# Norm of x at the head of an encoder block: transposing it by products with a scaled diagonal, squares on two engines, a TensorE run on zeros

## The chip, the core and the metric

The kernel runs on one core of one Trainium2 chip. The metric is the device time of one execution in microseconds. A core has five engines with instruction streams of their own: PE (TensorE, matmuls; its weight loads are shown as PEld), DVE (VectorE), ACT (ScalarE), POOL (GpSimd) and SP (SyncE, which here only issues DMAs). They meet in semaphores. SBUF is the on-chip memory of 128 partitions, PSUM (the tensor `ps`, 8 banks of 512 columns) takes what PE writes.

## What is computed

One encoder block for 256 tokens of width 2048, with 16 meta tokens put in front (272 rows, `L`): a norm, one wide projection, a state-space mixer and an attention mixer, their merge, and a feed-forward part that gathers rows of two tables for each token. What matters here is its first step:

```python
def rms_norm(x, g):
    xf = x.astype(jnp.float32)
    y = xf * lax.rsqrt(jnp.mean(xf * xf, axis=-1, keepdims=True) + NORM_EPS)
    return (y * g.astype(jnp.float32)).astype(x.dtype)

    hs = jnp.concatenate([meta, x], axis=1)
    h = rms_norm(hs, norm_mix[l])
    z = h @ w_in[l]
```

## The kernel before

**Layout.** x lies with tokens on the partitions: `xn` holds two halves of 128 tokens (t = 0, 1) with 2048 columns each, and the meta tokens are 16 rows of `xs`. The projection needs h turned round, with the model width on the partitions: 16 blocks `k` of 128 columns, each [128, 272]. It is needed in two parts, `hH` (rounded to what the fast matmul mode takes) and `hL` (the rest), so that three fast matmuls do the work of an exact one; weights are split in the same way into `high_slot(n)` and `low_ring`.

**The roots.** ACT squares the meta rows, the first half and the second half of x, each 2048 wide, and adds up in the same instruction (lines 480 to 487). DVE's `factors` makes the mean, ACT the root, DVE's `rstd` the reciprocal with one step of refinement: once for the meta rows and the first half together, once for the second half. DVE multiplies each half with its factor into `xs` (lines 880, 882), ACT the meta rows (line 491).

**The turn.** PE turns `xs` block by block: a transposition of the 16 meta rows (line 1321) and one for each half (line 1323), with `ident`, the identity of 128 x 128, into bank k % 4 of `ps`. ACT copies the bank to `hH` with the norm's weights (line 496), DVE makes `hL` of the bank and `hH` (line 887). A bank comes free when DVE is through with it.

**The first weights.** SP loads meta, the two halves of x, all parameters `prm` (128 x 1240, `ident` in their midst), and then weight tiles of 1 MB into a ring of four. ACT's `high(n)` (line 474) copies a ring slot rounded, DVE's `low(n)` (line 792) makes the rest; for tile 0 POOL does (line 401, `s_first`). ACT runs `high(0)` ahead of the turn and `high(1)` behind it. Then POOL makes two copies of h for later (lines 406, 407). PE's `split_product` (lines 1308 to 1310) takes 48 matmuls of 272 columns for a tile of 16 blocks and adds one to `s_wdone`, which SP's further loads and ACT's further `high` wait for.

**The order** is the order of the code on each engine; there is no scheduler. Programs of the engines wait for semaphore counts, written `wait_ge`. `step` on DVE makes an instruction wait for the one before.

Of the kernel before, what the change touches and what calls it, by code (L numbers as in the profile page):

```python
# [38 lines left out]
RING = 4  # L39
NEG = -3.0e38  # L40
# [25 lines left out]
def build(nc, W, keys, par, bw, cw, meta, x, gffn, gfin, u_tab, v_tab, out):  # L66
    top = ExitStack()
    with top:
        def sem(name):
            return top.enter_context(nc.semaphore(name))  # L70
# [24 lines left out]
        st = sbt(top, "st", [P, 16])  # L95
        halfpi = sbt(top, "halfpi", [P, 1])
# [66 lines left out]
        xs = gates[:, 0:3 * D].rearrange("p (t d) -> p t d", t=3)  # L163
        squares = [a[:, :, :].rearrange("p k t -> p (k t)") for a in (ybT, yT)]
# [65 lines left out]
        s_par = sem("s_par")  # L230
# [8 lines left out]
        s_sq, s_ms, s_sqr, s_xs = sem("s_sq"), sem("s_ms"), sem("s_sqr"), sem("s_xs")  # L239
        s_meta, s_xsm, s_gv = sem("s_meta"), sem("s_xsm"), sem("s_gv")  # L240
# [104 lines left out]
        def _(sp):  # L345
# [8 lines left out]
            sp.dma_start(xs[0:META, TT, :], meta).then_inc(s_x[TT], 16)  # L354
            for t in range(TT):
                sp.dma_start(xn[:, t, :], x[t * P:(t + 1) * P, :]).then_inc(s_x[t], 16)
            sp.dma_start(prm[:, :], par).then_inc(s_par, 16)
# [39 lines left out]
        def _(pool):  # L397
            pool.sem_inc(s_msum, 2)

            pool.wait_ge(s_high, 1)  # L400
            pool.tensor_tensor(low_ring[:, 0, :], ring[:, 0, :], high_slot(0), ALU.subtract).then_inc(s_first, 1)

            pool.wait_ge(s_hL, 4 + KT)
            pool.wait_ge(s_xs, TT)
            pool.wait_ge(s_sq, 3)
# [52 lines left out]
        def _(act):  # L458
            act.sem_inc(s_hT, 4)
# [20 lines left out]
            nc.scalar.activation(squares[0][0:META, :], xs[0:META, TT, :], ACT.Square, accum_out=st[0:META, 1:2]).then_inc(s_sq, 1)  # L480
            act.wait_ge(s_x[0], 16)
# [283 lines left out]
        def _(dve):  # L765
# [8 lines left out]
            dve.sem_inc(s_hL, 4)  # L774
# [9 lines left out]

            step(nc.vector.memset(halfpi[:, :], HALF_PI))
            step(nc.vector.memset(magic[:, :], MAGIC))
            nc.vector.memset(st[:, :], 1.0).then_inc(s_ms, 1)

            def low(n, i=0):

                dve.wait_ge(s_high, nth_high(n) + 1 + RING * i)
# [3 lines left out]
            def discretise():  # L795

                dve.wait_ge(s_par, 16)
# [62 lines left out]
            def rstd(dst, ss, v, root):  # L860
# [4 lines left out]
                step(nc.vector.tensor_scalar(ss, ss, -0.5, 1.5, ALU.mult, ALU.add))  # L865
# [3 lines left out]
            def factors(a, b, g):  # L869

                dve.wait_ge(s_sq, 2 + g)
                nc.vector.tensor_scalar(st[:, 3 + a:3 + b], st[:, a:b], 1.0 / D, EPS, ALU.mult, ALU.add).then_inc(s_ms, 1)
                dve.wait_ge(s_ms, 2 + g)
                dve.wait_ge(s_sqr, 1 + g)
                rstd(st[:, 9 + a:9 + b], st[:, a:b], st[:, 3 + a:3 + b], st[:, 6 + a:6 + b])
# [887 lines left out]
```

## Time and profile before

| | us |
|---|---|
| median of three runs | 2086.46 |
| lowest, highest | 2085.23, 2087.7 |
| the profiled execution | 2084.48 |
| its span, first to last instruction | 2082.6 |

The page gives PE 1768.3 us busy (85% of the span), DVE 1280.8, POOL 797.9, ACT 469.9. The core's DMA engines are busy for nine tenths and more from about a third of the span on, in the part that gathers rows. The chain of work that ended last is 50% PE and 32% DMA.

How to read the views: times are microseconds from the start of the span unless marked ns. The timeline lists instructions by start: start, duration, engine, line, operation, what is written and read, partitions x elements, how many were merged into the row (x), and in brackets the idle time before it with what ended it. Durations of matmuls overlap, because they are pipelined; their pace is the distance between starts. Granted clock (PEclk) is TensorE's clock as a share of 2.4 GHz.

### The profile page before, as it was taken

How to read it: one execution, taken by the hardware profiler on the slowest of the kernel's cores; microseconds unless marked ns; L12 is line 12 of the kernel's file. 1: busy time of each engine (PE TensorE's matmuls, PEld its weight loads, DVE VectorE, ACT ScalarE, POOL GpSimd, SP SyncE). 2: the span in 40 equal slices, each digit the busy share in tenths (PEclk: the TensorE clock that was granted, in tenths of full speed). 3: DMA queues.
4: the chain of work that ended last, by engine and by line, in shares of the span. 5: the costliest groups of instructions: out<-in, count | busy, mean ns of one | idle time of the engine just before them, and what ended most of it. 6: DMA issues, size and time to landing. Idle time of an engine off the chain costs nothing.

```text
span 2082.6 us, 24783 instructions
## 1 busy us (share of the span) xinstructions
PE 1768.3 (85%) x8224; PEld 1114.7 (54%) x8224; DVE 1280.8 (61%) x2427; ACT 469.9 (23%) x999; POOL 797.9 (38%) x711
## 2 busy tenths in 40 slices
PE   7999899998999999879979987777777777777776
PEld 5988798987998765425524532223332222222222
DVE  4534877784455355666566666666675665666654
ACT  5333565654434311011011010001000000000001
POOL 2022223331251034455455463444543543544432
PEclk9999899999999999999999999999999999999999
DMA  4487699997455589999999999999999999999997
GB/s 186 159 187 176 155 208 219 207 208 226 162 179 189 186 331 421 421 422 422 422 422 422 418 414 421 422 421 408 422 421 408 423 420 394 417 407 422 422 421 297
DMA packets 115893, 692.89 MB, mean 333 GB/s; under 512 B 12880, under 2 KB 12880, under 8 KB 41168
## 3 DMA queue, kind: packets, MB, share of 16 engines
q0 software_dynamic: 96768, 599.83, 76.4%
q1 hardware_dynamic: 19040, 92.00, 12.1%
q8 instruction: 45, 0.74, 0.1%
q14 instruction: 40, 0.33, 0.0%
HBM read 689.68 MB, written 2.10 MB: 332 GB/s over the span
## 4 chain that ended last, share of the span: by engine, by line
PE 50%; DMA 32%; issue 7%; DVE 6%; POOL 3%; ACT 1%; DVEq 0%; POOLq 0%; SPq 0%; ACTq 0%
DMA uv<-u_tab,eid 30%; PE ps L1666 15%; PE ps L1391 3%; PE ps L1396 3%; PE ps L1616 3%; PE ps L1397 3%; PE ps L1398 3%; PE ps L1493 2%; PE ps L1309 2%; PE ps L1310 2%; PE ps L1308 2%; POOL uv L454 2%; DVE uv L1246 2%; PE ps L1301 1%; PE ps L1600 1%
## 5 line engine op out<-in xcount | busy, mean ns | idle before, releaser
L1666 PE MATMUL ps<-uv,dg 128*128 128x512 f32 x2048 | 958.8, 614 | 267.3 <-DVE dg L1252 259.5
L1666 PEld LDWEIGHTS ps<-uv,dg 128*128 128x128 f32 x2048 | 381.1, 194 | 822.5 <-issue 472.4
L1246 DVE CUSTOM_DVE_ANT_0 uv<-uv,xn 128x2048 f32<-128x2048 f32 x256 | 587.2, 2294 | 378.4 <-DMA uv<-u_tab,eid 355.6
L454 POOL DMA_INDIRECT uv<-v_tab,eid x256 | 279.2, 1091 | 598.2 <-PE ps L1666 338.0
L451 POOL DMA_INDIRECT uv<-u_tab,eid x256 | 342.0, 1336 | 198.8 <-issue 183.9
L738 ACT ACTIVATE ga<-av 128x1 f32<-128x1 f32 x256 | 51.9, 203 | 1184.5 <-DVE av L1246 1180.7
L792 DVE TENSOR_TENSOR low_ring<-ring,wh 128x2048 fp32r<-128x2048 f32 x43 | 100.0, 2328 | 78.5 <-ACT wh L474 78.4
L1396 PE MATMUL ps<-hH,parts 128*128 128x256 f32 x480 | 146.1, 304 | 0.0
L424 POOL DMA_DIRECT2D parts<-W x80 | 69.9, 874 | 171.9 <-ACT parts L564 141.0
L1397 PE MATMUL ps<-hLx,parts 128*128 128x256 f32 x480 | 134.9, 281 | 0.0
L1398 PE MATMUL ps<-hH,parts 128*128 128x256 f32 x480 | 134.6, 280 | 0.0
L1252 DVE TENSOR_SCALAR dg<-prm,ga,gw 128x128 f32<-128x128 f32 x256 | 92.9, 363 | 67.1 <-ACT ga L738 32.6
L474 ACT ACTIVATE wh<-ring 128x2048 fp32r<-128x2048 f32 x44 | 84.4, 1919 | 134.0 <-PE ps L1310 101.8
L420 POOL DMA_DIRECT2D parts<-W x80 | 47.3, 591 | 171.2 <-PE ps L1398 101.8
L1616 PE MATMUL ps<-h2T,ring 128*128 128x256 f32 x448 | 100.8, 379 | 0.0
L1616 PEld LDWEIGHTS ps<-h2T,ring 128*128 128x128 f32 x448 | 85.1, 190 | 21.7 <-issue 11.5
L1396 PEld LDWEIGHTS ps<-hH,parts 128*128 128x128 f32 x480 | 90.4, 188 | 6.2 <-issue 5.2
L1397 PEld LDWEIGHTS ps<-hLx,parts 128*128 128x128 f32 x480 | 90.6, 189 | 1.0
L1398 PEld LDWEIGHTS ps<-hH,parts 128*128 128x128 f32 x480 | 90.4, 188 | 0.0
L1391 PE MATMUL ps<-xn,ring 128*128 128x256 f32 x320 | 76.4, 382 | 0.0
L564 ACT ACTIVATE parts<-parts 128x768 fp32r<-128x768 f32 x60 | 50.5, 841 | 108.1 <-DMA parts<-W 107.9
L1493 PE MATMUL ps<-uP,bwH 32*128 32x136 f32 x512 | 54.8, 319 | 9.0 <-DVE pb L1040 6.7
(282 smaller groups left out, 2313.1 us busy)
## 6 DMA issues: line engine op xcount, KB each, us to landing
ring<-W SPq DMA_DIRECT2D x64, 1024.0 KB
parts<-W POOLq DMA_DIRECT2D x160, 384.0 KB, 5.6
ring<-W SPq DMA_DIRECT2D x40, 256.0 KB, 5.2
xn<-x SPq DMA_DIRECT2D x4, 1024.0 KB, 10.5
uv<-u_tab,eid POOLq DMA_INDIRECT x256, 15.4
uv<-v_tab,eid POOLq DMA_INDIRECT x256
bwt<-bw SPq DMA_DIRECT2D x8, 256.0 KB, 6.3
cwt<-cw SPq DMA_DIRECT2D x8, 256.0 KB, 6.6
```

The costliest lines, as they stand in the source:

```text
L451: pool.indirect_dma_start(uv[:, s, 0, :], None, u_tab, at).then_inc(s_u[s], 16)
L454: pool.indirect_dma_start(uv[:, s, 1, :], None, v_tab, at).then_inc(s_vv[s], 16)
L792: nc.vector.tensor_tensor(low_ring[:, n % RING, :], ring[:, n % RING, :], high_slot(n), ALU.subtract).then_inc(s_low, 1)
L1246: nc.vector.tensor_tensor_reduce(uv[:, j % UV, 0, :], uv[:, j % UV, 0, :], xn[:, T, :], 1.0, 0.0, ALU.mult, ALU.add, av[:, hh, j:j + 1]).t ...
L1252: nc.vector.tensor_scalar(dg[:, j % 2, :], ident, ga[:, hh, j:j + 1], gw[:, hh, j:j + 1], ALU.mult, ALU.mult).then_inc(s_dg, 1)
L1391: nc.tensor.matmul(dst, whole(t)[:, k, :], hX[:, k, :], start=(k == 0), stop=False)
L1396: nc.tensor.matmul(dst, wh[:, m, :], hH[:, k, META:L], start=False, stop=False)
L1397: nc.tensor.matmul(dst, wh[:, m, :], hLx[:, k, :], start=False, stop=False)
L1398: ins = nc.tensor.matmul(dst, wl[:, m, :], hH[:, k, META:L], start=False, stop=(k == 2 * PART - 1))
L1493: ins = nc.tensor.matmul(ps[:, 2 + u, r * H2:(r + 1) * H2], w, x, start=(odd == 0 and part == 0), stop=(odd == 1 and part == 2))
L1616: ins = nc.tensor.matmul(ps[:, 4 + q % 2, 0:SEQ], w[:, k, :], h2T[:, k, :], start=(k == 0), stop=(k == KT - 1))
L1666: ins = nc.tensor.matmul(ps[:, 4 * T + n, :], dg[:, j % 2, :], uv[:, j % UV, 1, n * 512:(n + 1) * 512], start=False, stop=last and i == 2 ...
```

## The change

- DVE multiplies `ident` with the factors: `turners`, two diagonals of 128 x 128 and one of 16 x 16, in place of the scalings of x and of the meta rows. PE turns the unscaled x by ordinary matmuls with these diagonals as the moving operand, in place of transpositions.
- The blocks go through eight banks of `ps`, not four; the counters `s_hT` and `s_hL` start at 8.
- The squares of each half of x are shared: ACT takes the first 1024 columns, DVE the last 1024 (`tensor_tensor_reduce` into `sums`). One chain makes the factors of all three parts.
- PE begins with six matmuls (`WARMING`) of 128 x 512 on zeros that DVE has set; their result is not used.
- `ident` is loaded by a DMA of its own between the halves of x, the other parameters in two.
- `high(0)` and `high(1)` are made by two DMAs that POOL issues when the second half of x is there; DVE's and POOL's first `low` wait for them (`s_hd`). ACT's two copies are gone.
- POOL's copies of h wait for `s_low` 4, not for the turn.

```diff
-            sp.dma_start(prm[:, :], par).then_inc(s_par, 16)
+                if t == 0:
+                    sp.dma_start(prm[:, i0:i1], par[:, i0:i1]).then_inc(s_ident, 16)
+            sp.dma_start(prm[:, 0:i0], par[:, 0:i0]).then_inc(s_par, 16)
+            sp.dma_start(prm[:, i1:], par[:, i1:]).then_inc(s_par, 16)
...
-            pool.wait_ge(s_high, 1)
+            pool.wait_ge(s_x[TT - 1], 16)
+            for n in range(2):
+                pool.dma_start(high_slot(n), W[n, :, :]).then_inc(s_hd, 16)
+            pool.wait_ge(s_hd, 32)
+            pool.wait_ge(s_w[0], 16)
             pool.tensor_tensor(low_ring[:, 0, :], ring[:, 0, :], high_slot(0), ALU.subtract).then_inc(s_first, 1)
-            pool.wait_ge(s_hL, 4 + KT)
-            pool.wait_ge(s_xs, TT)
-            pool.wait_ge(s_sq, 3)
+            pool.wait_ge(s_low, 4)
...
-            nc.scalar.activation(squares[0], xn[:, 0, :], ACT.Square, accum_out=st[:, 0:1]).then_inc(s_sq, 1)
-            act.wait_ge(s_ms, 2)
-            nc.scalar.activation(st[:, 6:8], st[:, 3:5], ACT.Sqrt).then_inc(s_sqr, 1)
-            act.wait_ge(s_x[1], 16)
-            nc.scalar.activation(squares[1], xn[:, 1, :], ACT.Square, accum_out=st[:, 2:3]).then_inc(s_sq, 1)
-            act.wait_ge(s_ms, 3)
-            nc.scalar.activation(st[:, 8:9], st[:, 5:6], ACT.Sqrt).then_inc(s_sqr, 1)
-            act.wait_ge(s_meta, 1)
-            nc.scalar.activation(xs[0:META, TT, :], xs[0:META, TT, :], ACT.Copy, scale=st[0:META, 10:11]).then_inc(s_xsm, 1)
-            high(0, back=None)
+            for t in range(TT):
+                act.wait_ge(s_x[t], 16)
+                nc.scalar.activation(squares[0][:, t * D // 2:(t + 1) * D // 2], xn[:, t, 0:D // 2], ACT.Square, accum_out=st[:, t:t + 1]
+                                     ).then_inc(s_sq, 1)
+            act.wait_ge(s_ms, 2)
+            nc.scalar.activation(st[:, 6:9], st[:, 3:6], ACT.Sqrt, scale=1.0 / D).then_inc(s_sqr, 1)
+            act.wait_ge(s_par, 32)
...
-                nc.scalar.activation(hH[:, k, :], ps[:, k % 4, 0:L], ACT.Copy, scale=col("gmix", k, k + 1)).then_inc(s_hT, 1)
-            high(1)
+                nc.scalar.activation(hH[:, k, :], ps[:, k % 8, 0:L], ACT.Copy, scale=col("gmix", k, k + 1)).then_inc(s_hT, 1)
...
+            nc.vector.memset(warm, 0.0).then_inc(s_warm, 1)
...
+            for t in range(TT):
+                dve.wait_ge(s_x[t], 16)
+                nc.vector.tensor_tensor_reduce(squares[1][:, t * D // 2:(t + 1) * D // 2], xn[:, t, D // 2:], xn[:, t, D // 2:], 1.0, 0.0,
+                                               ALU.mult, ALU.add, sums[:, t:t + 1]).then_inc(s_half, 1)
+            dve.wait_ge(s_half, TT)
+            dve.wait_ge(s_sq, 1 + TT)
+            nc.vector.scalar_tensor_tensor(st[:, 3:6], st[:, 0:3], D * EPS, sums[:, :], ALU.add, ALU.add).then_inc(s_ms, 1)
+            dve.wait_ge(s_ms, 2)
+            dve.wait_ge(s_sqr, 1)
+            rstd(st[:, 9:12], st[:, 0:3], st[:, 3:6], st[:, 6:9], 1.0 / D)
+            dve.wait_ge(s_ident, 16)
+            for t in range(TT):
+                nc.vector.tensor_scalar(turners[t], ident, st[:, 9 + t:10 + t], None, ALU.mult).then_inc(s_turn, 1)
+            nc.vector.tensor_scalar(turners[TT], ident[0:META, 0:META], st[0:META, 11:12], None, ALU.mult).then_inc(s_turn, 1)
...
+            pe.wait_ge(s_warm, 1)
+            for _ in range(WARMING):
+                nc.tensor.matmul(ps[:, 0, :], warm[:, 0:P], warm, start=True, stop=True)
+            pe.wait_ge(s_turn, TT + 1)
             for k in range(KT):
...
-                nc.tensor.transpose(ps[:, k % 4, 0:META], xs[0:META, TT, c], ident[0:META, 0:META])
+                nc.tensor.matmul(ps[:, k % 8, 0:META], xs[0:META, TT, c], turners[TT], start=True, stop=True)
                 for t in range(TT):
-                    ins = nc.tensor.transpose(ps[:, k % 4, META + t * P:META + (t + 1) * P], xs[:, t, c], ident)
+                    ins = nc.tensor.matmul(ps[:, k % 8, META + t * P:META + (t + 1) * P], xn[:, t, c], turners[t], start=True, stop=True)
```

The order on POOL at the start of the program, before; `wh` is the rounded copy of a weight tile, `ring` the loaded one:

```order
L401 TENSOR_TENSOR low_ring<-ring,wh 128x2048 [waits s_high]
L406 TENSOR_TENSOR xn<-hH,hL 128x1024 [waits s_sq,s_xs,s_hL]
L407 COPY hLx<-hL 128x3072
L420 DMA parts<-W 128x768 [waits s_wdone] x2
L424 DMA parts<-W 128x768 [waits s_gn]
```

And of the change:

```order
L411 DMA wh<-W 128x2048 [waits s_x1]
L411 DMA wh<-W 128x2048
L414 TENSOR_TENSOR low_ring<-ring,wh 128x2048 [waits s_w0,s_hd]
L417 TENSOR_TENSOR xn<-hH,hL 128x1024 [waits s_low]
L418 COPY hLx<-hL 128x3072
L431 DMA parts<-W 128x768 [waits s_wdone] x2
```

Two DMAs now stand ahead of the first low part, which waits for both of them, and the copies of h wait for DVE's low parts.

The order on PE at the start, before; `gates` is the memory in which the scaled x lies, `prm` holds the identity:

```order
L1321 MATMUL ps<-prm,gates 128x16 [waits s_hT,s_xsm,s_hL,s_xs,s_par]
L1323 MATMUL ps<-prm,gates 128x128 x2
L1321 MATMUL ps<-prm,gates 128x16 [waits s_hL,s_hT]
L1323 MATMUL ps<-prm,gates 128x128 x2
L1321 MATMUL ps<-prm,gates 128x16 [waits s_hL,s_hT]
```

And of the change, where `gates` holds the diagonals and `trig` the zeros:

```order
L1328 MATMUL ps<-trig 128x512 [waits s_warm]
L1328 MATMUL ps<-trig 128x512 x5
L1335 MATMUL ps<-gates 128x16 [waits s_hL,s_hT,s_turn]
L1337 MATMUL ps<-gates,xn 128x128 x2
L1335 MATMUL ps<-gates 128x16 [waits s_hL,s_hT]
```

Six matmuls on zeros are put in front, and a block of the turn has the same three steps with other operands.

## Rows read from the trace of the kernel before

**Rows 1.** Waits of PE, 0 to 60 us: total, times, longest.
```profile
PE ps L1321 <- DVE gates L882: 14.0, 1, 14.0
PE ps L1308 <- DVE hL L887: 1.1, 1, 1.1
```
**Rows 2.** SP's line 356, the loads of x: issue ns and starts, landing.
```profile
L356 SPq DMA_DIRECT2D xn<-x x2: 411/418/424, 1.2 to 1.7; - x2
...
DMA to landing us min/median/max: 5.0/6.0/7.0
```
**Rows 3.** Timeline of ACT and DVE, 6 to 10 us.
```profile
6.23 1.91 ACT L483 ACTIVATE ybT<-xn 128x2048 f32<-128x2048 f32 x1 [0.68 <-DMA xn<-x]
8.05 0.19 ACT L483 ACTIVATION_READ_ACCUMULATOR ybT<-xn 128x1 f32 x1
8.35 0.17 DVE L872 TENSOR_SCALAR st<-st 128x2 f32<-128x2 f32 x1 [6.18 <-ACT ybT L483]
...
9.97 1.29 DVE L880 TENSOR_SCALAR gates<-xn,st 128x2048 f32<-128x2048 f32 x1
```
**Rows 4.** Timeline of PE and DVE: the turn's first and last block.
```profile
14.01 0.26 PE L1321 MATMUL ps<-prm,gates 16*128 16x16 f32 x1 [14.01 <-DVE gates L882]
...
26.48 0.28 PE L1321 MATMUL ps<-prm,gates 16*128 16x16 f32 x1
...
26.70 0.69 PE L1323 MATMUL ps<-prm,gates 128*128 128x128 f32 x2
...
27.94 0.50 DVE L887 SCALAR_TENSOR_TENSOR hL<-ps,prm,hH 128x272 fp32r<-128x272 f32 x1 [0.33 <-ACT hH L496]
```
**Rows 5.** Timeline of PE: the first product, and where its pace changes.
```profile
28.50 0.59 PE L1308 MATMUL ps<-hH,wh 128*128 128x272 f32 x1 [1.11 <-DVE hL L887]
...
33.42 0.43 PE L1308 MATMUL ps<-hH,wh 128*128 128x272 f32 x1
33.65 0.43 PE L1309 MATMUL ps<-hL,wh 128*128 128x272 f32 x1
...
34.07 0.29 PE L1308 MATMUL ps<-hH,wh 128*128 128x272 f32 x1
```
**Rows 6.** Timeline of POOL, DVE and ACT: the splitting of weights.
```profile
15.32 4.52 POOL L401 TENSOR_TENSOR low_ring<-ring,wh 128x2048 fp32r<-128x2048 f32 x1 [14.86 <-ACT wh L474]
...
29.74 3.31 DVE L792 TENSOR_TENSOR low_ring<-ring,wh 128x2048 fp32r<-128x2048 f32 x1 [1.30 <-ACT wh L474]
...
37.35 1.92 ACT L474 ACTIVATE wh<-ring 128x2048 fp32r<-128x2048 f32 x1 [7.64 <-PE ps L1310]
...
43.35 1.92 ACT L474 ACTIVATE wh<-ring 128x2048 fp32r<-128x2048 f32 x1 [3.80 <-PE ps L1310]
```
**Rows 7.** DVE: line 1246 (ns, starts), and a step on 64 columns.
```profile
L1246 DVE CUSTOM_DVE_ANT_0 uv<-uv,xn x256: 2281/2292/2358, 759.5 to 2067.9; 128x2048 f32<-128x2048 f32 x128
...
41.51 0.19 DVE L801 TENSOR_SCALAR gates<-prm 128x64 f32<-128x64 f32 x1
```
**Rows 8.** Timeline of PE, 135 to 136 us, fp32 products of the attention.
```profile
135.35 0.39 PE L1382 MATMUL ps<-pT,vr 128*128 128x128 f32 x2
135.67 0.48 PE L1383 MATMUL ps<-pT,vm 16*128 16x128 f32 x2
136.08 0.28 PE L1369 MATMUL ps<-prm,pr 128*16 128x128 f32 x1
```
**Rows 9.** Timeline of PE, 223 to 225 us: transpositions, then fp32 products.
```profile
222.93 1.12 PE L1453 MATMUL ps<-prm,hs 128*128 128x128 f32 x4
223.97 1.44 PE L1510 MATMUL ps<-hs,cp 128*64 128x129 f32 x12
```
**Rows 10.** Windows of PE: stretch, its length, busy (records), PEclk, DMA share, GB/s.
```profile
204.70:225.10 20.40, 12.22 (x122) 0.50 0.36 79
```
**Rows 11.** Timeline of PE: the first instruction after two stretches of idle time.
```profile
206.22 0.69 PE L1493 MATMUL ps<-uP,bwH 32*128 32x136 f32 x4 [2.36 <-DVE bwL L980]
...
116.93 1.18 PE L1358 MATMUL ps<-ukT,qT 128*128 128x272 f32 x4 [1.75 <-ACT qT L527]
```

More of the change, by code:

```diff
@@ L39 @@
 RING = 4
+WARMING = 6
 NEG = -3.0e38
@@ L95, in build @@
         st = sbt(top, "st", [P, 16])
+        sums = sbt(top, "sums", [P, 3])
         halfpi = sbt(top, "halfpi", [P, 1])
@@ L163, in build @@
         xs = gates[:, 0:3 * D].rearrange("p (t d) -> p t d", t=3)
+        turners = [xs[:, t, 0:P] for t in range(TT)] + [xs[0:META, 0, P:P + META]]
+        warm = trig[:, :, :, :, :].rearrange("p a b u t -> p (a b u t)")[:, 0:512]
         squares = [a[:, :, :].rearrange("p k t -> p (k t)") for a in (ybT, yT)]
@@ L225, in nth_low @@
             return n - 1 if n < W_Q else W_Q - 1 + n - W_PROJ
-        s_par = sem("s_par")
+        s_par, s_ident, s_warm = sem("s_par"), sem("s_ident"), sem("s_warm")
+        s_half, s_turn, s_hd = sem("s_half"), sem("s_turn"), sem("s_hd")
         s_x = [sem(f"s_x{t}") for t in range(TT + 1)]
@@ L238, in build @@
         s_trig0, s_f0 = sem("s_trig0"), sem("s_f0")
-        s_sq, s_ms, s_sqr, s_xs = sem("s_sq"), sem("s_ms"), sem("s_sqr"), sem("s_xs")
-        s_meta, s_xsm, s_gv = sem("s_meta"), sem("s_xsm"), sem("s_gv")
+        s_sq, s_ms, s_sqr = sem("s_sq"), sem("s_ms"), sem("s_sqr")
+        s_gv = sem("s_gv")
         s_hT, s_hL = sem("s_hT"), sem("s_hL")
@@ L458, in _ @@
         def _(act):
-            act.sem_inc(s_hT, 4)
+            act.sem_inc(s_hT, 8)
+            act.sem_inc(s_high, 2)
             act.sem_inc(s_uk, 2)
@@ L773, in _ @@
             dve.sem_inc(s_pm, 2)
-            dve.sem_inc(s_hL, 4)
+            dve.sem_inc(s_hL, 8)
             dve.sem_inc(s_hs, 4)
@@ L783, in step @@
                 dve.wait_ge(s_v, n_v[0])
+            nc.vector.memset(warm, 0.0).then_inc(s_warm, 1)
             step(nc.vector.memset(halfpi[:, :], HALF_PI))
             step(nc.vector.memset(magic[:, :], MAGIC))
+            step(nc.vector.memset(sums[:, 2:3], 0.0))
             nc.vector.memset(st[:, :], 1.0).then_inc(s_ms, 1)
             def low(n, i=0):
+                if n == 1:
+                    dve.wait_ge(s_hd, 32)
+                    dve.wait_ge(s_w[1], 16)
                 dve.wait_ge(s_high, nth_high(n) + 1 + RING * i)
@@ L795, in discretise @@
             def discretise():
-                dve.wait_ge(s_par, 16)
+                dve.wait_ge(s_par, 32)
                 d = [disc[:, k, :] for k in range(24)]
@@ L858, in discretise, with rstd @@
                 yield step(ins)
-            def rstd(dst, ss, v, root):
+            def rstd(dst, ss, v, root, unit=1.0):
                 step(nc.vector.reciprocal(dst, root))
@@ L864, in rstd @@
                 step(nc.vector.tensor_tensor(ss, ss, v, ALU.mult))
-                step(nc.vector.tensor_scalar(ss, ss, -0.5, 1.5, ALU.mult, ALU.add))
+                step(nc.vector.tensor_scalar(ss, ss, -0.5 * unit, 1.5, ALU.mult, ALU.add))
                 step(nc.vector.tensor_tensor(dst, dst, ss, ALU.mult))
[L869 to L875, printed above, removed]
@@ L885, in _ @@
+            nc.vector.tensor_scalar(turners[TT], ident[0:META, 0:META], st[0:META, 11:12], None, ALU.mult).then_inc(s_turn, 1)
+            dve.wait_ge(s_par, 32)
             for k in range(KT):
-                dve.wait_ge(s_hT, 4 + k + 1)
-                nc.vector.scalar_tensor_tensor(hL[:, k, :], ps[:, k % 4, 0:L], col("gmix", k, k + 1), hH[:, k, :],
+                dve.wait_ge(s_hT, 8 + k + 1)
+                nc.vector.scalar_tensor_tensor(hL[:, k, :], ps[:, k % 8, 0:L], col("gmix", k, k + 1), hH[:, k, :],
```

15 lines of the change are left out of this document (3 added, 12 removed).

## Prediction

> **What bounds the kernel now.** The page shows PE busy for most of the span and, from about a third of it on, DMA paced to the end; but the diff touches only the first microseconds. So the question is narrow: when does the first product with weights start, and how fast does it run. From there on everything is released by PE's own progress (the ring's loads, ACT's `high`, DVE's `low` and POOL's casts wait for `s_wdone` or for one another), so a microsecond won or lost ahead of it should stand at the end as one microsecond. I read the waits of PE first: there are two in the first 60 us, 14.0 us for the scaled x and 1.1 us for the last low part of h [rows 1]. Then the timeline, where three stretches follow one another.
>
> *The roots.* x lands in two halves, 5.0 and 7.0 us after issues at 1.2 and 1.7, at 6.2 and 8.7 [rows 2]. ACT squares each half whole, a chain of small steps runs for each, and DVE scales both; PE starts at 14.01 [rows 3, 4].
>
> *The turn.* 16 blocks of one small and two full transpositions. The first begins at 14.01 and the last at 26.48, so 0.83 us a block, of which the small one takes 0.21; the last ends at 27.39, 13.4 us in all. DVE needs 0.50 of each 0.83 [rows 4] (ACT as much), so PE paces this, and four banks are enough.
>
> *The first product.* It starts at 28.50, 1.11 after the turn. Its matmuls of 272 columns come every 0.23 us until the rise near 33.9, then at the pace that a whole tile of 48 has later: 6.00 us between two of ACT's `high`, 0.125 each [rows 5, 6]. These are the two levels of TensorE's clock, 1.2 and 2.4 GHz (the page's clock digit says 9 here only because no record of it lies ahead of the rise). The first tile ends at about 37.3, where ACT's next `high` is released. So 13.4 us of transpositions at 1.2 GHz didn't raise the clock, and 5.4 us of products back to back did.
>
> **The change, part by part.**
>
> *Roots.* ACT squares half a row: (8.05 - 6.23)/2 + 0.19 = 1.1 us [rows 3]. DVE's half is the instruction of line 1246, 2.29 for 2048 elements, so 1.15 for 1024, plus 0.1 to read the sum [rows 7]. The second half of x lands a little later (64 KB of the diagonal go ahead of it: at the 2.45 us that a MB of x took, 0.15), at 8.85, so both sums stand at 10.1. From the sums to the factors is 8.35 to 9.97 as now, 1.62 [rows 3], plus 0.1 for one more wait: 11.85. Three diagonals take the place of two scalings of 2048; 64 columns take 0.19 [rows 7], so 0.2 each: 12.45. PE can start at 12.45 in place of 14.01, **-1.55**, bounds -1.0 and -2.0.
>
> *The turn as products.* A product in fp32 leaves two records where a transposition leaves one (lines 1382 and 1383 are listed x2 for one product each) [rows 8]. At 2.4 GHz a pair of 128 columns streams in 0.22: one record of 129 columns takes half of 0.21 there. But each block changes between 16 rows and 128, which isn't free: from line 1382 to the 16-row product is 0.32, and from that to the next 0.41 [rows 8]. With 16 columns moving in place of 128 I take 0.32 for the small one, since its second weight load covers the difference in part. A block at 2.4 GHz is then 0.32 + 0.32 + 0.32 = 0.95 us (bounds 0.66, without any cost of the changes, and 1.05), the turn 15.3: 1.9 us *more* than now. At 1.2 GHz a full record takes 0.21 more for each that is added (line 1510, six in turn in the 1.44 us of its twelve, two of them side by side; line 1453, four in the 1.04 us up to it) [rows 9]. Today's block has three records and 0.83; the two further full ones make +0.43, the second small one with its load +0.1 to +0.25, slower weight loads up to +0.2. Bounds 1.26 and 1.7; I take 1.55, as each of the three is seen to cost something: the turn 24.8, **+11.4**. ACT and DVE need 0.5 a block, so eight banks in place of four buy nothing while PE paces.
>
> *Zeros.* Six products of 512 columns are 12 records of 4 x 0.21 = 0.85 at 1.2 GHz [rows 9], 10.2 us in all, and half a microsecond less for each one after a rise. The stream begins near 2.5 and, with a rise 3.5 to 6 us in (5.4 was seen at 28.50, and I estimate that it varies with where the stream begins), ends between 9.4 and 10.7. The diagonals come at 12.45: PE is idle for 2 to 3 us just ahead of the turn.
>
> *Does the clock hold?* After a gap of 2.36 us at 206.22, with four transpositions and another gap ahead of it, PE ran slow, and PEclk is 0.50 from 204.7 to 225.1 [rows 10, 11]. After 1.75 us at 116.93 it ran on fast (four records of 272 columns in 1.18) [rows 11]. A gap of 2 to 3 us and then a turn full of small pauses lies nearer to the first. And once down, what would raise it? A turn at 1.2 GHz is the stream of 14 to 27 again, with more columns in each block but the same two changes of rows, and that stayed down for 13.4 us. I take it that the clock is down when the turn begins, or soon after, and stays down.
>
> The Trainium skill, "TensorE: Matmul & The Clock Gate", Part 4, says that transposes in transpose mode do not count as busy for the clock in the way that products do. By that rule the stretch from 14 to 27 says nothing of products and the turn would raise the clock by itself, which is rival 1 and some 2 us *less* than now. The trace agrees in that stretch; but the rise at 225.1 came with a microsecond of transpositions (line 1453) just ahead of it [rows 9, 10], so it doesn't settle the matter.
>
> *The first product in the changed kernel.* With the clock down at its start it is today's, 8.7 us, a rise near 5 us in: -0.1. With the clock up it takes 6.0: -2.7.
>
> *Weights.* `high(0)` and `high(1)` leave ACT for two DMAs that POOL issues after x. ACT's copies were off the path, so this wins nothing. The cost: the first `low`, 4.5 us on POOL [rows 6], now waits for both. Ahead of and with them 9.2 MB are to land, at 2.45 us a MB: by 24.5 at the worst, by 21 where the two queues share, so `s_first` is up by 29 or 25.5. The first product is ready at 28.9 with the clock up and at 38.3 with it down: nothing. POOL's copies of h move from 28.5 to behind `low(4)`; DVE's `low` beside them takes 3.31 [rows 6], and with ACT's 1.92 ahead of it that is 5.2 of the 6.0 that a tile has: nothing. SP issues two more DMAs ahead of the weights, under the transfers: nothing.
>
> **The sum:** -1.55 + 11.4 - 0.1 = **+9.75**. The profiled execution took 2084.48 us (2082.6 of span and 1.9 around it), which gives 2094.2; it lay 2 us under the median 2086.46, and against that, which I forecast, it is 2096.2. A measurement tells about 0.2% (4.2 us) from no change.
>
> **The rivals.**
> 1. *The clock is up in the turn*, kept through the gap or raised by the products soon after. -1.55 + 1.9 - 2.7 = -2.3, or about -0.9 where some 3.5 us of the turn run low (at 1.55 in place of 0.95 a block, 1.4 us more): 2084.1 to 2085.6. For it: the skill's rule, and more columns in each block than now. Against it: the gap, the pauses, and the 13.4 us. It decides in the first blocks, 0.95 us apart or 1.55. This is the case on the other side: not slower.
> 2. *The clock is up and most of the changes of rows are hidden:* a block of 0.72, the turn 11.5, so -1.55 - 1.9 - 2.7 = -6.1, 2080.4. Rows 8 speak against it.
> 3. *The wait for the copied weights takes over.* It needs rival 2's turn and the DMAs late: the product starts at 28, with the clock up, -0.5 - 2.7 = -3.2: 2083.3.
> 4. *The clock is down, but a block takes 1.26:* -1.55 + 6.8 - 0.1 = +5.2: 2091.6, a part of the forecast's own range.
>
> **How the numbers follow.** Clock down for all or most of the turn, rival 4 included: 0.54. Rival 1: 0.34, within 0.2%. Rivals 2 and 3: 0.12, of which 0.10 are faster by over 0.2%. So faster 0.10, same 0.36, slower 0.54. The range must take in rival 1, so its low end is 2083.0 (2084.1 less the spread of the runs, 1.2); blocks of 1.7 give 27.2 and +12.2, 2098.7, and I take 2098.5. The likeliest case's own range is 2091 to 2098.5.
>
> **What would show it.** In the profile after, the zeros run from near 2.5 to near 10, then PE idles for 2 to 3 us; the turn starts between 12.0 and 13.0 (else the roots' term is wrong); its blocks are 1.55 us apart (forecast), 0.95 (rival 1) or under 0.8 (rival 2); the first product of 272 columns starts near 38 with matmuls every 0.23 for 3 to 6 us (rival 1: near 29, every 0.125). The wait ahead of it names DVE's `hL`; if it names POOL's `low_ring`, rival 3 is there. From the second tile on the traces differ by a constant. The forecast is wrong if the blocks are closer than 1.2 us.

## The result, and the profile after

| | before | after |
|---|---|---|
| median | 2087.31 | 2094.69 |
| lowest, highest of 20 | 2084.24, 2091.8 | 2083.47, 2098.69 |
| the profiled execution | 2084.48 | 2093.26 |
| its span | 2082.6 | 2091.4 |

The ratio of after to before is 1.0029, with a 95% interval of 1.0019 to 1.0039. The medians lie 7.4 us apart (1.0035) and the profiled executions 8.8; the ratio is not that of the medians, here or below. The changed kernel is slower.

Its 20 times are not one cloud but two groups. Three stand at 2083.47, 2084.12 and 2084.92, and 17 between 2093.03 and 2098.69, with nothing in the eight microseconds between. The mean granted clock of TensorE over the execution was 0.976 to 0.978 in the three and 0.969 to 0.974 in the 17. The profiled execution is one of the 17. Its stretch of 26 us at half the clock (below) takes about 0.006 from a mean over 2091 us, and that is the distance between the two groups' means, 0.977 and 0.971 (a single execution is less sure a sign: the ten of w8, below, read 0.974 to 0.978). None of the three was profiled.

The waits of PE after, first 60 us (columns: who waited, for whom, us in total, times, longest). They answer to rows 1, where there were two; the 14.0 us ahead of the turn have become two waits with the zeros between them:

```profile
PE ps L1328 <- DVE trig L791: 2.5, 1, 2.5
PE ps L1335 <- DVE gates L894: 1.9, 1, 1.9
PE ps L1320 <- DVE hL L899: 1.1, 1, 1.1
```

The timeline of PE after. Line 1328 is the run on zeros, 1335 the product for the meta rows, 1337 those for the two halves (x4 is two products), 1320 to 1322 the first product with weights. It answers to rows 4 and 5:

```profile
2.49 8.12 PE L1328 MATMUL ps<-trig 128*128 128x512 f32 x12 [2.49 <-DVE trig L791]
12.51 0.39 PE L1335 MATMUL ps<-gates 16*128 16x16 f32 x2 [1.90 <-DVE gates L894]
...
13.47 0.39 PE L1335 MATMUL ps<-gates 16*128 16x16 f32 x2
...
14.43 0.39 PE L1335 MATMUL ps<-gates 16*128 16x16 f32 x2
...
15.90 0.60 PE L1335 MATMUL ps<-gates 16*128 16x16 f32 x2
...
17.59 0.60 PE L1335 MATMUL ps<-gates 16*128 16x16 f32 x2
...
36.14 0.60 PE L1335 MATMUL ps<-gates 16*128 16x16 f32 x2
36.68 1.22 PE L1337 MATMUL ps<-gates,xn 128*128 128x128 f32 x4
39.02 0.59 PE L1320 MATMUL ps<-hH,wh 128*128 128x272 f32 x1 [1.11 <-DVE hL L899]
...
41.67 0.43 PE L1322 MATMUL ps<-hH,low_ring 128*128 128x272 f32 x1
...
42.12 0.29 PE L1321 MATMUL ps<-hL,wh 128*128 128x272 f32 x1
```

The granted clock over the same stretches (columns: stretch, its length, busy with the records, granted clock, share of the DMA engines, GB/s):

```profile
10.20:12.50 2.30, 0.41 (x1) 1.00 0.99 413
12.50:15.00 2.50, 2.49 (x15) 0.96 1.03 419
15.40:41.80 26.40, 25.29 (x93) 0.50 0.36 145
```

The column of the clock reads 1.00 for everything ahead of a trace's first rise, because no record of the clock lies there: in run w0 below it reads 1.00 for 12.4 to 37.7, where the blocks are 1.69 apart. There the pace tells, not the column.

What to see. The zeros ran at 2.4 GHz when they ended near 10.6. PE then idled for 1.90 us. The turn began at 12.51 and its first two blocks take 0.96 each, still at 2.4 GHz. Within the third, of 1.47, the clock fell to 1.2 GHz, and from 15.90 on the blocks are 1.69 apart, 13 of them. The turn ends at 37.9, 25.4 us in all where it was 13.4. The clock rises only near 42, some 3 us into the first product with weights.

Where it stands further down: ACT's first rounded copy that waits for PE's tile starts at 46.79 where it was 37.35 [rows 6], +9.4:

```profile
46.79 1.92 ACT L486 ACTIVATE wh<-ring 128x2048 fp32r<-128x2048 f32 x1 [8.36 <-PE ps L1322]
```

The lag does not stay at 9.4. At the sixth tile with weights it grows by 1.0, and the first line here is before, the others after:

```profile
53.58 0.73 DVE L808 TENSOR_TENSOR gates<-gates 128x64 f32<-128x64 f32 x3
63.07 5.33 DVE L819 TENSOR_TENSOR gates<-gates 128x64 f32<-128x64 f32 x3
63.23 2.40 POOL L417 TENSOR_TENSOR xn<-hH,hL 128x1024 f32<-128x1024 f32 x1 [34.45 <-DVE low_ring L803]
71.50 0.39 PE L1320 MATMUL ps<-hH,wh 128*128 128x272 f32 x1 [0.73 <-DVE low_ring L803]
```

POOL's copies of h now run from 63.23 to 68.33. In that time three small steps of DVE take 5.33 us in place of 0.73; the low part behind them comes late, and PE waits 0.73 us for it where the kernel before doesn't wait. ACT's copy of `ukT` is 9.5 us late behind the fifth tile and 10.6 behind the sixth. All ten traces with the copies at the new place show 5.32 to 5.35 for these steps, and the three that have them behind the turn (bz10, b_grp, bz10_grp) 0.74. No run moves the copies alone. After that the lag moves between about 8 and 13 us (9.8 at 150, 10.7 near 257, 9.3 near 308) and is 8.8 at the end of the span.

### The profile page after: what moved, and what is told of

Its sections match the earlier page's. It is cut to its first block and busy times, and to the rows that moved or that the text cites. A ratio compares the mean times of both kernels' runs of the same rounds, so it can differ in the third digit from the quotient of the medians.

```text
span 2091.4 us, 24905 instructions
## 1 busy us (share of the span) xinstructions
PE 1790.9 (86%) x8284; PEld 1130.3 (54%) x8284; DVE 1285.8 (61%) x2428; ACT 462.1 (22%) x995; POOL 798.2 (38%) x713
## 5 line engine op out<-in xcount | busy, mean ns | idle before, releaser
L465 POOL DMA_INDIRECT uv<-v_tab,eid x256 | 274.8, 1073 | 596.4 <-PE ps L1680 340.4
L462 POOL DMA_INDIRECT uv<-u_tab,eid x256 | 347.8, 1358 | 199.5 <-issue 185.2
L1405 PEld LDWEIGHTS ps<-xn,ring 128*128 128x128 f32 x320 | 58.3, 191 | 7.7 <-issue 0.3
```

Source lines behind the costliest of these rows:

```text
L462: pool.indirect_dma_start(uv[:, s, 0, :], None, u_tab, at).then_inc(s_u[s], 16)
L465: pool.indirect_dma_start(uv[:, s, 1, :], None, v_tab, at).then_inc(s_vv[s], 16)
L1405: nc.tensor.matmul(dst, whole(t)[:, k, :], hX[:, k, :], start=(k == 0), stop=False)
```

## The experiments

What was open: whether the idle time ahead of the turn took the clock down, and not the products themselves; why a turn at 1.2 GHz doesn't raise it; and what the parts on weights and banks do. Each ratio is against executions of the kernel before on the same chip, whose medians were 2086.96 to 2087.28. w8, w0, bz10 and w8_grp shared a chip, z6_late, w8_act, w8_b4 and w8_grp_act a second, the other four a third, and the changed kernel has its own 20 executions of before. What is compared across these groups goes by the ratios; a trace shows one execution of its kernel.

**1. Two more products on zeros (w8).**

```diff
-WARMING = 6
+WARMING = 8
```

> The changed kernel with eight matmuls on zeros in place of six. Theory (TensorE's clock decides; it falls in the turn because PE idles for 1.9 us ahead of it): the zeros end near 12.2, the gap is under 0.5 us, the clock stays up through the turn, blocks are 0.96 apart throughout, the first product starts near 29 and runs at 0.125 a matmul: about 2 us under the kernel before in every run, 2085, and 10 under the changed kernel. Rival (the turn as products can't hold the clock, gap or no gap): blocks go to 1.69 after a few, as in the changed kernel, and the time is again near 2094.

Measured: 2083.26 (2080.88 to 2086.22, ten), ratio 0.9983, interval 0.9973 to 0.9992. Two more products of work that nobody uses made the changed kernel 11.4 us faster, and faster than before. The timeline of PE and a window over its turn:

```profile
2.49 9.68 PE L1328 MATMUL ps<-trig 128*128 128x512 f32 x16 [2.49 <-DVE trig L791]
12.77 0.39 PE L1335 MATMUL ps<-gates 16*128 16x16 f32 x2 [0.59 <-DVE gates L894]
...
13.73 0.39 PE L1335 MATMUL ps<-gates 16*128 16x16 f32 x2
...
27.19 0.39 PE L1335 MATMUL ps<-gates 16*128 16x16 f32 x2
...
29.34 0.39 PE L1320 MATMUL ps<-hH,wh 128*128 128x272 f32 x1 [1.11 <-DVE hL L899]
```

```profile
12.00:29.00 17.00, 15.63 (x97) 1.00 0.77 312
```

The idle time is 0.59 in place of 1.90, all 16 blocks are 0.96 apart, and the first product starts at 29.34 at 0.125 a matmul. This is rival 1 in full.

**2. The same six, begun later (z6_late).** w8 changes two things, the length of the run on zeros and the gap behind it. Here the length stays and only the gap goes: PE begins the six when ACT's squares of the meta rows are done.

```diff
             pe.wait_ge(s_warm, 1)
+            pe.wait_ge(s_sq, 1)
             for _ in range(WARMING):
```

> The changed kernel with its six matmuls on zeros, but PE begins them only when ACT has squared the meta rows (near 5.5 us), not near 2.5. Theory (the idle gap ahead of the turn drops the clock, not the number of zeros): the zeros end between 12.2 and 14, there is no gap, the clock stays up, blocks 0.96 apart, no execution near 2094; the time is that of w8 plus 0 to 1.5 us, 2083 to 2085. Rival (six are too few, it takes eight): the clock falls in the turn as in the changed kernel, 2092 to 2095.

Measured: 2083.69 (2082.07 to 2086.7, ten), ratio 0.9984, interval 0.9974 to 0.9993. PE:

```profile
5.85 7.46 PE L1329 MATMUL ps<-trig 128*128 128x512 f32 x12 [5.85 <-ACT ybT L492]
13.24 0.39 PE L1336 MATMUL ps<-gates 16*128 16x16 f32 x2
```

No bracket stands behind 13.24: the turn follows the zeros at once, the blocks are 0.96 apart to the last. So it is the gap and not the number of products, and none of the ten executions lies above 2086.7. The turn starts 0.7 late, because the zeros hold it up, and this costs little beside the 12.

**3. No zeros (w0).** Would the turn, without any help, raise the clock?

```diff
-            nc.vector.memset(warm, 0.0).then_inc(s_warm, 1)
...
-            pe.wait_ge(s_warm, 1)
-            for _ in range(WARMING):
-                nc.tensor.matmul(ps[:, 0, :], warm[:, 0:P], warm, start=True, stop=True)
```

> The changed kernel without any matmul on zeros. Theory: the turn begins at 1.2 GHz and its blocks, 1.69 apart, never raise it: the turn takes 27 us, the time is 2096, 1 to 2 us over the changed kernel. Rival (products raise the clock by themselves where transpositions did not): blocks go from 1.69 to 0.96 within 7 us, and the time is 2087 to 2089.

Measured: 2095.38 (2094.95 to 2097.52, five), ratio 1.0039, interval 1.0025 to 1.0054. PE:

```profile
12.41 0.61 PE L1330 MATMUL ps<-gates 16*128 16x16 f32 x2 [12.41 <-DVE gates L893]
...
37.71 0.60 PE L1330 MATMUL ps<-gates 16*128 16x16 f32 x2
...
40.58 0.59 PE L1319 MATMUL ps<-hH,wh 128*128 128x272 f32 x1 [1.11 <-DVE hL L898]
```

From 12.41 to 37.71 there are 15 blocks of 1.69: 27 us of products, none of which raised the clock. The median of the changed kernel's slower group, 2095.1, is 0.3 us from that of no zeros at all: in 17 executions of 20 the zeros did little. In the traces they did more (the first tile with weights ends 2.7 us later here), but this one is the slowest of its five, at 2097.52.

**4. The old turn behind zeros (bz10).** The kernel before with ten products on zeros, which end just ahead of its first transposition, and nothing else.

```diff
+            nc.vector.memset(warm, 0.0).then_inc(s_warm, 1)
...
+            pe.wait_ge(s_warm, 1)
+            for _ in range(10):
+                nc.tensor.matmul(ps[:, 0, :], warm[:, 0:P], warm, start=True, stop=True)
```

> The kernel before with ten matmuls on zeros ahead of its turn by transpositions, nothing else. Theory: transpositions count like products, only with less in them. The clock is up when the turn starts at 14.0; a block of transpositions at 2.4 GHz should take about 0.55 (0.10 a full record, the rest changes of rows), and if it holds, the first product starts near 24 and fast: 7 us under the kernel before. Rival (transpositions do not count for the clock at all): it falls within some 4 us of the turn's start, the rest of the turn is at 0.83 a block, and the gain is 1 to 3 us.

Measured: 2083.04 (2078.89 to 2085.66, ten), ratio 0.9977, interval 0.9967 to 0.9986. PE, and two windows:

```profile
14.12 0.20 PE L1326 MATMUL ps<-prm,gates 16*128 16x16 f32 x1 [0.51 <-DVE gates L884]
...
14.62 0.23 PE L1326 MATMUL ps<-prm,gates 16*128 16x16 f32 x1
...
17.61 0.28 PE L1326 MATMUL ps<-prm,gates 16*128 16x16 f32 x1
...
18.44 0.28 PE L1326 MATMUL ps<-prm,gates 16*128 16x16 f32 x1
```

```profile
14.00:17.00 3.00, 2.68 (x16) 1.00 1.01 421
17.40:30.80 13.40, 12.29 (x48) 0.50 0.15 62
```

At 2.4 GHz a block of transpositions takes 0.50 to 0.53, at 1.2 GHz 0.83 as in rows 4. The clock held for the first six blocks and then fell, though the gap was only 0.51. So the old turn, interleaved as it is, loses the clock where w8's products after a gap of 0.59 held it. Whether that is the transpositions or their pauses isn't parted: PE is busy for 2.68 of the 3.00 us here, and ahead of the fifth block it waits 0.20 us for ACT to free one of the four banks, where w8's turn has no such wait. Even so this one edit gives as much as w8 with all of the change.

**5. The small products of four blocks first (w8_grp),** with eight products on zeros. The eight banks allow it. It takes the 32 changes between 16 and 128 rows down to 8.

```diff
-            for k in range(KT):
...
+            for g in range(KT // 4):
+                for k in range(4 * g, 4 * g + 4):
...
                     nc.tensor.matmul(ps[:, k % 8, 0:META], xs[0:META, TT, c], turners[TT], start=True, stop=True)
+                for k in range(4 * g, 4 * g + 4):
...
+                  ins.then_inc(s_tr, 1)
```

> As w8, and the small products of four blocks run together ahead of the eight full ones, so that PE changes between 16 and 128 rows 8 times and not 32. Theory (a change of rows costs 0.1 us each way and a fresh weight load): a block falls from 0.96 to about 0.65, the turn from 15.3 to 10.5, and the first product then waits for POOL's first low part, which ended at 28.8 in the changed kernel: start 28.9, no gain over w8 in the time, and the wait names low_ring. Rival (rows cost nothing, PE paces by something else): blocks stay at 0.96.

Measured: 2084.51 (2082.68 to 2086.33, ten), ratio 0.999, interval 0.998 to 0.9999. PE:

```profile
12.46 1.06 PE L1336 MATMUL ps<-gates 16*128 16x16 f32 x8 [0.88 <-DVE gates L894]
13.45 2.05 PE L1340 MATMUL ps<-gates,xn 128*128 128x128 f32 x16
15.43 1.06 PE L1336 MATMUL ps<-gates 16*128 16x16 f32 x8
...
28.59 0.56 PE L1320 MATMUL ps<-hH,wh 128*128 128x272 f32 x1 [4.17 <-issue]
```

Four blocks take 2.97, 0.74 each (0.65 had been expected), so grouping won 0.22 a block and the turn was 3.5 us shorter. The kernel became no faster. PE waited 4.17 us ahead of the first product, and the view puts this down to "issue", that is, to nothing it knows. POOL's timeline tells it:

```profile
23.99 4.50 POOL L414 TENSOR_TENSOR low_ring<-ring,wh 128x2048 fp32r<-128x2048 f32 x1 [13.41 <-DMA wh<-W]
```

It ends at 28.49, and the product starts at 28.59. This is rival 3: the wait for the copied weights has taken over, and by the start of the product the clock had fallen too, so that the first tile ends 1.6 us later than w8's (37.31 against 35.74):

```profile
27.30:33.60 6.30, 5.01 (x22) 0.50 0.00 0
```

**6. The same with the weights' part undone (w8_grp_act).** ACT makes `high(0)` behind the roots and `high(1)` behind the turn, as before the change; POOL's two DMAs are gone, and with them DVE's wait for them.

```diff
-            pool.wait_ge(s_x[TT - 1], 16)
-            for n in range(2):
-                pool.dma_start(high_slot(n), W[n, :, :]).then_inc(s_hd, 16)
-            pool.wait_ge(s_hd, 32)
-            pool.wait_ge(s_w[0], 16)
+            pool.wait_ge(s_high, 1)
...
+            high(0, back=None)
             act.wait_ge(s_par, 32)
...
+            high(1)
```

> As w8_grp (eight matmuls on zeros, small products in fours), with the weights part of the change undone: ACT rounds tile 0 ahead of the turn and tile 1 behind it, POOL waits for that and no longer for two DMAs. Theory (the 4.2 us that PE stood idle ahead of the first product in w8_grp were the wait for POOL's first low part): low 0 is there by 20, the first product starts 1.1 us after the turn, near 25.5, at 2.4 GHz from its first matmul; 3.5 to 4 us under w8, 2079 to 2080. Rival (the turn in fours doesn't hold the clock, or ACT's extra 1.9 us delays the turn): start later than 27, or the first product slow, no better than w8.

Measured: 2080.21 (2078.29 to 2081.28, five), ratio 0.9964, interval 0.9951 to 0.9978. The first product:

```profile
25.55 0.39 PE L1314 MATMUL ps<-hH,wh 128*128 128x272 f32 x1 [1.11 <-DVE hL L893]
```

Three microseconds earlier than with the DMAs, named to `hL` again, and at 2.4 GHz. As soon as the turn is short enough, the part on weights costs 3.0 us at the start of the first product and, with the clock that the gap takes down, 5.4 at the end of the first tile (37.31 against 31.96). At the medians it is 4.3, on two chips; the intervals of the two ratios do not meet.

**7. Weights' part undone alone (w8_act)**, with the turn block by block and eight zeros: 2083.63 (2081.47 to 2085.3, ten), ratio 0.9986, interval 0.9976 to 0.9995, against 2083.26 of w8.

> w8 with only the weights part undone (ACT rounds tiles 0 and 1, no DMAs from POOL, small products not grouped). Theory (ACT has the time, and the first low part was ready at 28.8 just ahead of the first product at 29.3): start and time as w8, within 0.7 us, 2083. Rival (the two copies by DMA save something on the path): 1 to 2 us slower than w8.

The first product started at 28.92, 0.4 earlier than in w8, because the zeros ended earlier and the turn began at 12.35 in place of 12.77. `low_ring` is ready at 28.8 in the changed kernel (24.27 + 4.52 on POOL), just under that: behind a turn of 15.4 us the DMAs cost nothing that can be measured, and win nothing.

**8. Four banks (w8_b4)**, k % 4 in place of k % 8, with eight zeros: 2083.37, ratio 0.9987, interval 0.9973 to 1.0001.

> w8 with four banks of PSUM in the turn in place of eight. Theory (PE paces the turn, ACT and DVE need 0.5 us of 0.96): the same, within 0.5 us of w8, 2083. Rival (PE waits for banks): idle time of PE ahead of the small products, named hL, and blocks over 0.96.

Blocks 0.96 apart and no wait for a bank: eight banks buy nothing while the turn goes block by block, as PE paces. Nine of the ten times are 2081.85 to 2085.38 and one is 2096.45. Here PE had idled for 1.29 us ahead of the turn:

```profile
12.48 0.39 PE L1335 MATMUL ps<-gates 16*128 16x16 f32 x2 [1.29 <-DVE gates L894]
```

That one execution lies where the 17 of the changed kernel lie, and its mean granted clock, 0.973, is the lowest of the ten (the others 0.976 to 0.981). I take it for a turn that lost its clock; it was not the profiled one, so this isn't shown. The profiled one held the clock through the whole turn and lost it in the first product, from 29.6 to 33.0 (0.50 for 29.7 to 32.9), although that product began at 2.4 GHz and PE did not pause: its first tile took 7.9 us where w8's took 6.4. Only the idle times of 1.29 and 1.11 us ahead of turn and product came before.

**9. Nine on zeros, grouped, ACT's weights (w9_grp_act)**, the combination that should close the gap for good: 2079.49 (2078.14 to 2083.76, six), ratio 0.9967, interval 0.9955 to 0.9979. Turn from 12.42 with no idle time ahead, first product at 25.49.

> w8_grp_act with nine matmuls on zeros in place of eight, so that PE hardly idles ahead of the turn. Theory: the zeros end between 11.9 and 13.1, the turn starts up to 0.6 us later than 12.5 in some executions, never finds the clock down; the median is that of w8_grp_act within 0.7 us, 2080 to 2081, and no execution lies above 2085. Rival (the idle time of 1.4 us in w8_grp_act costs something in many executions): the median is 1 us or more lower.

Against w8_grp_act's idle 1.45 us, this brought nothing that can be told apart (2079.49 against 2080.21, intervals overlapping); in the profiled execution there the clock had held.

**10. Grouped, no zeros (w0_grp_act).** w0 left open whether products can't raise the clock or their pauses keep it down. Same turn as in 9, without the zeros. Against w0 two things differ, the order of the products and the weights' part; w8_act has shown that the second leaves the pace of the turn as it is.

> w8_grp_act without any matmul on zeros: the turn in fours, from the clock at 1.2 GHz. It tells what kept the clock down in w0. If it is the pauses and row changes between the products (theory): this turn has a quarter of them, a block takes about 1.3 us at 1.2 GHz, and the clock rises within about 7 us, after which a block takes 0.74; first product near 28 to 31, time 2083 to 2087. If products of this kind never raise the clock (rival): blocks of 1.3 to the end, first product near 34.5, time 2089 to 2091.

Measured: 2084.32 (2081.84 to 2086.4, ten), ratio 0.9988, interval 0.9979 to 0.9997. PE:

```profile
12.43 1.88 PE L1325 MATMUL ps<-gates 16*128 16x16 f32 x8 [12.43 <-DVE gates L887]
14.24 3.47 PE L1329 MATMUL ps<-gates,xn 128*128 128x128 f32 x16
17.64 1.06 PE L1325 MATMUL ps<-gates 16*128 16x16 f32 x8
...
20.61 1.06 PE L1325 MATMUL ps<-gates 16*128 16x16 f32 x8
```

The first four blocks took 5.21, the next four the 2.97 of a turn at 2.4 GHz. The same products in another order raise the clock about 5 us in, where those of w0 did not in 25. So it was the alternation of 16 and 128 rows that kept it down. That it does so by pauses is my reading: the view shows none in w0 (PE busy for 25.29 of 25.30 us), and only the longer blocks speak for them.

**11 and 12. The transpositions grouped (b_grp, bz10_grp).** The kernel before, its turn in fours through eight banks in the manner of 5, without zeros and with ten.

```diff
-                nc.tensor.transpose(ps[:, k % 4, 0:META], xs[0:META, TT, c], ident[0:META, 0:META])
-                for t in range(TT):
...
+            for g in range(KT // 4):
+                for k in range(4 * g, 4 * g + 4):
...
+                    nc.tensor.transpose(ps[:, k % 8, 0:META], xs[0:META, TT, c], ident[0:META, 0:META])
+                for k in range(4 * g, 4 * g + 4):
...
+                    ins.then_inc(s_tr, 1)
```

> The kernel before with its transpositions in fours (four small ones, then eight full ones) through eight banks, no zeros, nothing else. It tells whether transpositions count for the clock. Theory (what counts is how little PE pauses; w0_grp_act's products raised the clock once grouped): a four takes about 2.4 us at 1.2 GHz in place of 3.3, the clock rises within 7 us, then ACT and DVE pace at 0.5 a block; first product near 23 and fast: 7 to 8 us under the kernel before. Rival (the skill's rule: transpositions don't count): 2.4 us a four to the end, the clock at 1.2 until 5 us into the first product; first product near 25, 3.5 us under the kernel before.

> b_grp with the ten matmuls on zeros of bz10 ahead of the turn, so that the clock is up when it starts. Theory (grouped transpositions keep the clock up): blocks at 0.5 us, paced by ACT and DVE, first product near 23.3 at 2.4 GHz, 8 us under the kernel before, near 2079. Rival (transpositions don't count): the clock falls within 4 us of the turn's start as in bz10, the first product near 24 starts at 1.2 GHz, 4 to 5 us under the kernel before.

Measured: b_grp 2082.4 (2079.62 to 2083.89, seven), ratio 0.9978, interval 0.9966 to 0.9989; bz10_grp 2079.14 (2076.58 to 2080.86, five), ratio 0.9955, interval 0.994 to 0.997. PE of b_grp (line 1322 the small ones, 1326 the full ones of four blocks):

```profile
14.08 0.64 PE L1322 MATMUL ps<-prm,gates 16*128 16x16 f32 x4 [14.08 <-DVE gates L882]
14.65 1.97 PE L1326 MATMUL ps<-prm,gates 128*128 128x128 f32 x8
16.55 0.60 PE L1322 MATMUL ps<-prm,gates 16*128 16x16 f32 x4
...
18.82 0.41 PE L1322 MATMUL ps<-prm,gates 16*128 16x16 f32 x4
...
20.19 0.41 PE L1322 MATMUL ps<-prm,gates 16*128 16x16 f32 x4
...
23.57 0.39 PE L1308 MATMUL ps<-hH,wh 128*128 128x272 f32 x1 [1.95 <-DVE hL L887]
```

The first group took 2.47, the third 1.37: pure transpositions raised the clock within the turn, near 18.7, and the first product starts at 23.57 at full pace, where the kernel before started at 28.50 at half of it. Its profiled execution, 2079.83, is 2.6 under the median, so not every execution need look like this. The time misses its theory of 7 to 8 us: 4.9 at the medians. In the traces the lead is 7.4 us at the end of the first tile and 4.7 at the end of the span; it melts between 230 and 1400 us, and no run says why.

PE's windows of bz10_grp:

```profile
15.50:16.50 1.00, 1.00 (x10) 0.89 0.99 410
16.50:17.50 1.00, 1.00 (x6) 0.50 1.01 418
...
19.50:20.50 1.00, 1.00 (x10) 0.90 0.00 0
```

The clock fell in the second group, after 0.93 us of idle time ahead of the turn, and rose again in the fourth. In this execution it was down once more at the start of the first product (from 22.97, after 1.69 us of idle time) and up near 26.4. It has the lowest median of this study, 8.1 us under that of the kernel before (9.4 by the ratio), without a product by a diagonal, without the roots' part, the copied weights and the moved copies of h. Its interval overlaps those of w8_grp_act and w9_grp_act, so it is level with them and not shown to be faster. What its zeros win over b_grp, 3.3 us at the medians, the two traces don't show: there its first tile ends 0.9 us later (30.89 against 29.98), and its profiled execution is the slowest of five.

## Why the prediction was right, and where it was off

The forecast was 2096.2 and the median is 2094.69; the likeliest case came out, and for the reason given. That the two are only 1.5 us apart is in part luck: the forecast was +9.75 on three runs' median of 2086.46, the measured change +7.4 on a median of 2087.31. Its steps in turn:

**The roots: right.** -1.50 measured (12.51 against 14.01), -1.55 forecast. The diagonals came at 12.5 where 12.45 was worked out.

**Zeros: right.** They ended at 10.6, within the 9.4 to 10.7 forecast, and PE idled for 1.90, just under the "2 to 3 us".

**Does the clock hold: right in the main, and not certain in the way that the text left open.** "The clock is down when the turn begins, or soon after, and stays down": it was down from the third block on, for the whole turn. That the first blocks were still fast (0.96, 0.96 and 1.47, not 1.69) was not in the sum; it is -1.7. The reason given, that a turn at 1.2 GHz with its changes of rows would not raise the clock, was the weakest step, since it was read from transpositions and carried over to products. Runs w0 and w0_grp_act bear it out: it is the changes of rows. And rival 1, at 0.34, is no mere might-have-been. The three executions at 2083.5 to 2084.9 stand at its 2084.1 and among those of w8 and z6_late, whose traces are rival 1's; that the three are turns which kept the clock is likely and not shown, since none was profiled.

**The block: under-sized.** At 1.2 GHz it is 1.69, forecast 1.55, at the upper bound of 1.7. From 15.90 to 16.44 is 0.54 for the small product, where it took 0.32, and the rest, 1.15, is 0.575 for each full one, where it took 0.32. So each part of a block grows by a factor of 1.7 to 1.8 with the clock, the changes of rows too; the estimate had let these keep most of their time. At 2.4 GHz it is 0.96, forecast 0.95. The turn: 0.96 + 0.96 + 1.47 + 13 x 1.69 = 25.4, +12.0 in place of +11.4. Of two errors, -1.7 for the first blocks and +2.2 for 16 blocks at 0.14 more, 0.6 was left: the sum was nearer than its terms.

**The first product: off by 1 us.** It was to be "today's", with a rise near 5 us in. It started at 39.02, and the rise came 3 us in. So it took 1.1 us less than before in place of 0.1. In w0_grp_act and in rows 5 the rise came about 5 us in; nothing in these runs says which it will be.

**Sum of the measured terms:** -1.50 + 12.0 - 1.1 = +9.4, which is what ACT's copies show at the end of the first tile. That a microsecond there would stand at the end as one, and that the traces would differ by a constant from the second tile on, holds only within 2 us or so: 10.6 behind the sixth tile, 8.8 at the end, and b_grp's lead of 7.4 shrinks to 4.7. The profiled execution of after lies 1.4 under its median and that of before 2.8 under its own, and 8.8 + 1.4 - 2.8 = 7.4, the difference of the medians.

**Weights: right for this kernel.** The wait ahead of the first product names `hL`. The last of the two DMAs landed at 24.1, between the 21 and the 24.5 given, and `low_ring` was up at 28.8. Rival 3 came true in w8_grp, at the price of 3 to 4 us, and the text had put its condition rightly: a shorter turn.

**POOL's copies of h: wrong, and unseen in the total.** They were put at nothing, because DVE's `low` beside them takes 3.31 and fits into a tile. It was not the low part that they ran beside but DVE's small steps ahead of it, 5.33 us in place of 0.73, and behind the sixth tile the kernel is 1.0 us later for it. All kernels with products by a diagonal carry this; the three on the kernel before do not.

**Rival 1's size: not contradicted.** It was given -2.3 with the clock up all through. w8's trace has the end of the first tile at 35.74 against 37.35, -1.6, and the end of the span at -2.0; its ratio gives -3.6 us, with an interval of -5.6 to -1.7. Trace and ratio differ because the profiled execution of before is a fast one of its kernel (2.8 under the median) and that of w8 lies only 0.8 under its own.

**Of rows and pages.** The prediction set a rule of the Trainium skill, "TensorE: Matmul & The Clock Gate", Part 4, against rows 4: transposes in transpose mode do not count as busy for the clock as products do. What the runs show is first that interleaved transpositions lose the clock (bz10) where interleaved products keep it (w8), each after a gap of half a microsecond; the rule agrees with that much. But interleaved products never raise it (w0), and grouped transpositions do (b_grp, near 18.7, 4.6 us into pure transpositions). There the rule, as stated, does not hold, and the measurement decides. That the two differ in degree only, and that the changes of rows weigh more, is my reading of it.

**What stays open.** What makes one execution in some keep the clock: gaps of 1.45 (w8_grp_act) and 1.95 us (b_grp, behind transpositions) were survived in the profiled executions, gaps of 1.90 (after) and 0.93 us (bz10_grp) were not, and the changed kernel's times fall in two groups. The gap need not be the same in each execution either: the same eight products on zeros took 9.68 us in w8's trace, 9.34 in w8_act's, 9.09 in w8_grp's, 8.70 in w8_b4's and 8.54 in w8_grp_act's, so the gap behind them went from 0.5 to 1.45 us. The three fast executions of the changed kernel may have had a shorter gap, or the same one and survived it; no trace tells. Not tried: the diagonals without the shared squares, so the roots' 1.5 us were never timed by themselves; and the copies of h at their old place in a kernel with diagonals.

## What to carry to other kernels

A run on zeros ahead of real work is worth what it does to the gap behind it: look whether the real work begins without idle time and keeps PE busy, and if a time comes in two groups, compare their granted clocks before anything else. Group small matmuls with another number of rows apart from full ones, since here each change cost time and the stream that alternated didn't raise the clock. When work off the path is moved, look which steps of other engines it will then run beside. When a stage gets shorter, look again at each wait that it had hidden, and where the view blames "issue" for a gap, look on the other engines for what ended just there.

## What the runs showed of the hardware

- The same 48 products of a turn at 1.69 us a block never raised the clock in 25 us; in another order, with 8 changes between 16 and 128 rows in place of 32, they raised it in about 5 us (w0, w0_grp_act).
- Going from 16 rows to 128 and back costs, at 2.4 GHz, 0.22 us of each block's 0.96 beyond what one group of four pays (0.74).
- At 2.4 GHz a block of one small and two full transpositions takes 0.50 to 0.53 alternating and 0.34 in fours (1.37 for four); of products by a diagonal in fp32 0.96 and 0.74. So the products cost twice as much as the transpositions, and only their hold on the clock (w8 against bz10) speaks for them.
- Of the changed kernel, 17 executions have a median of 2095.1 and 3 one of 2084.1, with mean granted clocks of 0.969 to 0.974 and 0.976 to 0.978. The profiled one of the 17 lost the clock behind an idle time of 1.90 us. With a gap of 0.59 or none in the profiled execution (w8, z6_late) all twenty executions stay under 2086.8.
- While POOL's two copies of h ran, three DVE steps of 64 columns took 5.33 us in place of 0.73 (after and before; ten traces against four).
- Two 1 MB DMAs of weights that POOL issued at 9.3 to 10.6, beside SP's loads, landed by 24.1.
